# Eight key slabs of the input projection move into the paged-attention stage, and each ring slab becomes one transfer

## What is computed

```python
h = h + 0.5 * swiglu_1(rms_norm(h))              # d_ff 5632
u = rms_norm(h) @ w_in                           # q | k | v | conv value and gate
A = differential attention with ALiBi, 8 heads   # prompt, and samples over paged K and V
B = GLU -> causal depthwise conv (31 taps) -> group LayerNorm -> swish
h = h + concat(A, B) @ w_out
h = h + 0.5 * swiglu_2(rms_norm(h))
h = h + (p @ w_ple_proj) * sigmoid(rms_norm(h) @ w_ple_gate)
y = rms_norm(h)                                  # k, v and conv state are outputs too
```

## Time and profile before

| | us |
|---|---|
| median of 3 runs (2712.27 to 2714.64) | 2712.81 |
| the profiled execution, its own time | 2711.31 |
| its span, from the first to the last instruction | 2709.5 |
| first FFN and the 16 dense slabs of `w_in` | 0 to 1066 |
| attention stage | 1066 to 1514.7 |
| output projection, second FFN, the rest | 1514.7 to 2709.5 |

### The profile page before, as it was taken

One profiled execution on the slowest core, in us unless ns is written; L12 is line 12 of the kernel. 1 busy time (PEld: TensorE's weight loads), 2 busy tenths in 40 slices (PEclk: granted clock), 3 DMA queues, 4 the chain that ended last, 5 costly groups with the idle time before them and its releaser, 6 DMA issues.

```text
span 2709.5 us, 49989 instructions
## 1 busy us (share of the span) xinstructions
PE 2611.9 (96%) x20082; PEld 2542.3 (94%) x20082; DVE 1497.4 (55%) x2082; ACT 942.0 (35%) x1075; POOL 354.3 (13%) x630
## 2 busy tenths in 40 slices
PE   7999999999999999988887899999999999999997
PEld 7999999999999999977775899999999999999997
DVE  5555555555555644467786345555555555555655
ACT  5222322223222332354555433222222222222433
POOL 2000000000000120066865010000000000000323
PEclk9999999999999999999999999999999999999998
DMA  5444444444444455799999844444444444444342
GB/s 231 156 143 152 155 141 153 146 149 154 145 149 152 142 185 200 284 377 365 377 375 382 305 155 144 152 150 145 155 147 147 154 142 153 151 143 155 140 145 81
DMA packets 92112, 506.37 MB, mean 187 GB/s; under 512 B 10401, under 2 KB 10402, under 8 KB 51298
## 3 DMA queue, kind: packets, MB, share of 16 engines
q1 hardware_dynamic: 90866, 496.59, 50.5%
q0 software_dynamic: 1136, 8.32, 0.9%
HBM read 495.63 MB, written 9.23 MB: 186 GB/s over the span
## 4 chain that ended last, share of the span: by engine, by line
PE 89%; DMA 3%; ACT 2%; SPq 2%; issue 2%; POOL 1%; DVE 1%; POOLq 0%; DVEq 0%; ACTq 0%
PE bank L1589 26%; PE bank L1590 26%; PE bank L1591 26%; PE bank L1675 2%; PE bank L1677 2%; PE bank L1676 2%; DMA raw<-k_pool 2%; PE bank L1715 1%; PE bank L1764 1%; SPq L427 1%; POOL ssq L518 1%; SPq L422 1%; PE bank L1741 1%; ACT x_hi L666 1%; DMA raw<-v_pool 1%
## 5 line engine op out<-in xcount | busy, mean ns | idle before, releaser
L1589 PE MATMUL bank<-x_hi,w_hi 128*128 128x320 f32 x3584 | 1111.6, 310 | 17.0 <-DVE w_lo L1046 10.9
L1590 PE MATMUL bank<-x_lo,w_hi 128*128 128x320 f32 x3584 | 1109.9, 310 | 0.0
L1591 PE MATMUL bank<-x_hi,w_lo 128*128 128x320 f32 x3584 | 1109.7, 310 | 0.0
L1037 DVE TENSOR_TENSOR w_lo<-raw,w_hi 128x2048 fp32r<-128x2048 f32 x309 | 707.7, 2290 | 305.8 <-ACT w_hi L648 291.0
L648 ACT CAST w_hi<-raw 128x2048 fp32r<-128x2048 f32 x294 | 559.6, 1903 | 838.2 <-PE bank L1591 838.2
L1589 PEld LDWEIGHTS bank<-x_hi,w_hi 128*128 128x128 f32 x3584 | 674.9, 188 | 19.0 <-issue 13.6
L1590 PEld LDWEIGHTS bank<-x_lo,w_hi 128*128 128x128 f32 x3584 | 675.1, 188 | 0.2
L1591 PEld LDWEIGHTS bank<-x_hi,w_lo 128*128 128x128 f32 x3584 | 674.9, 188 | 0.0
L1589 PE MATMUL bank<-mid_hi,w_hi 128*128 128x320 f32 x1408 | 435.3, 309 | 1.0 <-DVE w_lo L1037 1.0
L1591 PE MATMUL bank<-mid_hi,w_lo 128*128 128x320 f32 x1408 | 435.1, 309 | 0.0
L1590 PE MATMUL bank<-mid_lo,w_hi 128*128 128x320 f32 x1408 | 435.1, 309 | 0.0
(11 more groups left out here) (215 smaller groups left out, 2011.7 us busy)
## 6 DMA issues: line engine op xcount, KB each, us to landing
raw<-slabs_ffn SPq DMA_DIRECT2D x264, 1024.0 KB, 4.7
raw<-k_pool SPq DMA_DIRECT2D x128, 512.0 KB, 6.5
raw<-v_pool SPq DMA_DIRECT2D x128, 512.0 KB, 6.4
raw<-slabs_in SPq DMA_DIRECT2D x48, 512.0 KB, 7.8
raw<-slabs_ple SPq DMA_DIRECT2D x18, 1024.0 KB, 4.8
raw<-slabs_in SPq DMA_DIRECT2D x16, 1024.0 KB, 4.8
raw<-slabs_out SPq DMA_DIRECT2D x16, 1024.0 KB, 4.8
h<-x_t SPq DMA_DIRECT2D x4, 640.0 KB, 8.1
```

What stands on the lines that cost most here:

```text
L1037: vt.tensor_tensor(w_lo[n % 2][:, :, :], raw[n % 4][:, :].rearrange("p (k n) -> p k n", n=P), w_hi[n % 2][:, :, :].bitcast(F32), ALU.subtr ...
L1589: mm(out, w_hi[w2][:, t, :], xh, start=start, stop=False)
L1590: mm(out, w_hi[w2][:, t, :], xl, start=False, stop=False)
L1591: return mm(out, w_lo[w2][:, t, :], xh, start=False, stop=stop)
```

## The change

The dense part of `w_in` keeps only the 8 query slabs (`N_PRE` = 8). The 8 key slabs become the slabs of iteration 0, the 8 value slabs those of iteration 1, two a step, and the convolution and the prompt heads start at iteration 2: `position` counts from there, so that triple c = 0 begins at (2, 0), and block 7 is gated at (7, 3) and not at (6, 3). Iteration 1 therefore has `score(1, q)`, two slabs, the value transposes, `turn(0, q)` and `weigh(0, q)`. The banks of slabs alternate between D_BANK and G_BANK, and value tiles are transposed into H_BANK alone. The casts of finished convolution blocks and heads for the output projection move from iteration 7 to iteration 8, and block 7 gets a piece of its own, `conv_c`, after the split of the first `w_out` slab. That slab ("O") is loaded behind all values and no longer ahead of the last two. GpSimd's key output and `queries(2)`, `queries(3)` shift with the rest. In the ring a slab is loaded by one DMA of 8 KB per partition, with one wait; SP sets the second semaphore of the slot itself.

```diff
-N_PRE = 16
+N_PRE = 8
...
-    if it == 0:
-        return (2 * q, 2 * q + 1)
-    c, r = divmod(4 * (it - 1) + q, PERIOD)
-    return (8 + 2 * c + r,) if c < 8 and r < 2 else ()
+    if it < 2:
+        return (8 * it + 2 * q, 8 * it + 2 * q + 1)
+    c, r = divmod(4 * (it - 2) + q, PERIOD)
+    return (16 + 2 * c + r,) if c < 8 and r < 2 else ()
...
-                if it == NB and q == GROUPS - 1:
-                    order.append(("O", 0))
                 order += [("V", KV_SLOTS * (it - 1) + 2 * q + e) for e in range(2)]
-    return order
+    return order + [("O", 0)]
...
-                    for e in range(2):
-                        slot_free(n, e)
-                        sp.dma_start(ring[slot][:, 1024 * e:1024 * e + 1024],
-                                     slabs_in[N_PRE + at, :, 1024 * e:1024 * e + 1024]
-                                     ).then_inc(ring_in[slot][e], 16)
+                    slot_free(n, 1)
+                    sp.dma_start(ring[slot][:, :], slabs_in[N_PRE + at, :, :]).then_inc(ring_in[slot][0], 16)
+                    sp.sem_inc(ring_in[slot][1], 16)
...
-            pool.wait_ge(evacuated, E(S_IN + 15))
+            pool.wait_ge(d_read, HEADS)
             pool.dma_start(k_t, kT[:, :, :]).then_inc(stored, 16)
...
                     if (it, q) == (NB, 3):
                         sample_upper(0, "sample_a")
                         slab_upper(0)
+                        conv_upper(7, 8, "conv_c")
...
                     if (it, q) == (NB, 3):
+                        conv_swish(7)
                         sample_lower(0, "sample_a")
                         slab_lower(0)
+                        conv_lower(7, 8, "conv_c")
...
+            for q in range(GROUPS):
+                score(1, q)
+                if q:
+                    turn(0, q)
+                slab_half(8 + 2 * q, 0)
+                if q == 0:
+                    turn(0, q)
+                slab_half(8 + 2 * q, 1)
                 if q:
                     v_turn(2 * q - 1)
-                v_slab(2 * q + 1)
+                slab_whole(9 + 2 * q)
                 v_turn(2 * q)
+                if q < GROUPS - 1:
+                    weigh(0, q)
+                if q == 1:
+                    turn(0, "new")
+            score_new(1)
             v_turn(7)
-            score_new(0)
-            for it in range(1, NB + 1):
+            weigh(0, 3, (0,))
+            weigh_new(0)
+            weigh(0, 3, (1,))
+            for it in range(2, NB + 1):
```

More of the change, by code:

```diff
@@ L609, in _ @@
             queries(2)
+            queries(3)
             for c in range(8):
                 sample_taps(c)
-                if c in (0, 1, 2, 4, 5):
-                    queries({0: 3, 1: 4, 2: 5, 4: 6, 5: 7}[c], c + 1)
+                if c in (0, 1, 2, 4):
+                    queries({0: 4, 1: 5, 2: 6, 4: 7}[c], c + 1)
             pool.wait_ge(ln_done, 8)
@@ L728, in _ @@
                     root(1)
-            with act.Fori(1, 3) as i:
-                for j in range(4):
-                    split_next(S_IN, i, j)
             for j in range(3):
-                split_next(S_IN, 3, j)
+                split_next(S_IN, 1, j)
             def exp_tables():
@@ L744, in half_up @@
                 e = n % 2
-                act.wait_ge(ring_in[slot][e], full)
+                act.wait_ge(ring_in[slot][0], full)
                 if n < WBUF:
@@ L760, in v_copy @@
                 nc.scalar.copy(vtok[:, :, P * j:P * j + P],
-                               (H_BANK if j % 2 else G_BANK)[:, 0:3 * P].rearrange("p (a n) -> p a n", n=P)
+                               H_BANK[:, 0:3 * P].rearrange("p (a n) -> p a n", n=P)
                                ).then_inc(vtok_done, 1)
@@ L893, in _ @@
                 slab_up(2 * q + 1)
+                slab_up(2 * q + 2)
+            exp_scores(0, (0,))
+            for q in range(GROUPS):
+                if q == 2:
+                    copy_ET(0, "new")
+                slab_up(9 + 2 * q)
+                copy_ET(0, q)
+                exp_scores(0, ((1, 4), (2,), (3,), ())[q])
                 if q:
                     v_copy(2 * q - 1)
-                slab_up(2 * q + 2)
+                slab_up(10 + 2 * q)
                 v_copy(2 * q)
             v_copy(7)
-            exp_scores(0, (0,))
-            for it in range(1, NB + 1):
+            exp_scores(1, (0,))
+            for it in range(2, NB + 1):
                 b = it - 1
@@ L1161, in _ @@
                 for j in range(4):
-                    split_next(S_IN, i, j)
+                    if not (i == 1 and j == 3):
+                        split_next(S_IN, i, j)
                     if i == 0 and j == 2:
@@ L1168, in _ @@
                         query_tile(i, j)
[L1169 to L1175, removed]
             def tables():
@@ L1403, in _ @@
                 slab_low(2 * q + 1)
-                read_v(2 * q)
+                read_k(2 * q)
                 slab_low(2 * q + 2)
-                read_v(2 * q + 1)
+                read_k(2 * q + 1)
             read_new(0)
             maxima(0)
+            for q in range(GROUPS):
+                if q == 0:
+                    slab_low(9)
+                read_scores(1, q)
+                if q:
+                    slab_low(9 + 2 * q)
+                read_v(2 * q)
+                slab_low(10 + 2 * q)
+                read_v(2 * q + 1)
+            inverse_sums(0)
+            read_new(1)
+            maxima(1)
             dve.wait_ge(state_in, 16)
@@ L1650, in _ @@
                     sum_features(1)
-            with pe.Fori(1, 4) as i:
-                for j in range(4):
-                    pe.wait_ge(evacuated, E(S_IN + 4 * i + j - 4))
-                    dense(S_IN + 4 * i + j, j, j)
+            for j in range(4):
+                pe.wait_ge(evacuated, E(S_IN + j))
+                dense(S_IN + 4 + j, j, j)
             pe.wait_ge(consts, 2)
@@ L1678, in half_of, with slab_half, slab_whole @@
                 m.then_inc(half_mm, 1)
-            def v_slab(j):
-                if j >= 2:
-                    pe.wait_ge(d_read, j - 1)
-                for e in range(2):
-                    half_of(2 * j + e, (O_BANK if j % 2 else D_BANK)[:, 0:NTOK])
+            def slab_half(k, e):
+                if e == 0 and k >= 2:
+                    pe.wait_ge(d_read, k - 1)
+                half_of(2 * k + e, (G_BANK if k % 2 else D_BANK)[:, 0:NTOK])
+            def slab_whole(k):
+                slab_half(k, 0)
+                slab_half(k, 1)
             def conv_half(n):
                 if n % 2 == 0:
-                    c = (n // 2 - HEADS) // 2
+                    c = (n // 2 - 2 * HEADS) // 2
                     pe.wait_ge(d_read, n // 2)
@@ L1694, in v_turn @@
             def v_turn(j):
-                pe.wait_ge(d_read, j + 1)
-                if j >= 2:
-                    pe.wait_ge(vtok_done, j - 1)
-                elif j == 1:
+                pe.wait_ge(d_read, HEADS + j + 1)
+                if j:
+                    pe.wait_ge(vtok_done, j)
+                else:
                     pe.wait_ge(cchain, 6)
-                out = H_BANK if j % 2 else G_BANK
                 for a, t0 in enumerate((0, P, NTOK - P)):
-                    e = nc.tensor.transpose(out[:, P * a:P * a + P], tmp[j % 2][:, t0:t0 + P], ident[:, :])
+                    e = nc.tensor.transpose(H_BANK[:, P * a:P * a + P], tmp[j % 2][:, t0:t0 + P], ident[:, :])
                 e.then_inc(v_turned, 1)
@@ L1747, in o_part, with weigh @@
                 return O_BANK[32 * j:32 * j + 32, at:at + P]
-            def weigh(b, g):
-                if g == 0:
-                    if b == 0:
-                        pe.wait_ge(d_read, HEADS)
-                    else:
-                        pe.wait_ge(o_read, 2 * b)
+            def weigh(b, g, parts=(0, 1)):
+                if g == 0 and b:
+                    pe.wait_ge(o_read, 2 * b)
                 pe.wait_ge(et_done, 10 * b + TURN_AT[g] + 2)
-                for e2 in range(2):
+                for e2 in parts:
                     values = arrived(("V", KV_SLOTS * b + 2 * g + e2))
```

111 lines of the change are left out of this document (61 added, 50 removed).

## The result

The changed kernel takes 2718.22 us (median of 12 runs, 2716.12 to 2722.82), the kernel before 2713.81 in the same runs (12, 2709.54 to 2717.46): ratio 1.0020, 95% interval 1.0013 to 1.0028. That is 4.4 us slower, where 2712.0 was forecast. The profiled execution took 2716.81 us, its span is 2715.0; before, 2711.31 and 2709.5.

What follows compares the result with a forecast made beforehand. TensorE was taken to bound the dense part and iteration 0, DMA transfers the attention after it. Terms -55.6 - 2.5 + 80.9 - 2 + 1.5 - 23.1 = -0.8 us gave a median of 2712.0, range 2699 to 2722.

Steps and rivals of the forecast that it cites:

- The start of attention: With the key slabs out of the dense part, attention starts at 1010.4 and not 1066.01: -55.6 us.
- iteration 1: The value slabs' iteration, new in attention: TensorE sets the pace in steps of 19.7 us, +80.9 us in all.
- its sign of being wrong: In iteration 8, ScalarE's serial stretch being shorter or longer than 12 us would show the forecast wrong.
- The single transfer: Ring slabs behind iteration 1, loaded by one DMA of 8 KB per partition: +1.5 us, with ends of -6 and +7.
- both rivals built on it: Ring slabs: one transfer fills the queue, -10.5, 2702, chance 0.18; or its first half is late, +9, 2722, chance 0.25.
- the one in which the transfers alone set the end: Tail: block 7's taps do not hold it, the last landing does; -42 there, sum -20, 2693 us, chance 0.07.
- the rival at 2722: Ring slabs: ScalarE's upper half waits for the whole slab, TensorE behind it; +4.7 up to +9 us, chance 0.25.
- term 1: Key slabs leave the dense part: -55.6 us, with two query copies of about 0.24 and waits, 0.8 us, exposed.
- term 6: Tail, block 7's gating to output projection: GpSimd's taps 29.3 plus 21.0 us behind them, 50.3 against 73.4, -23.1.
- iteration 0: Key slabs replace value slabs, without value transposes: bare steps of 16.3 us, 66.1 in all against 68.64, -2.5.
- The head start: Iterations 2 to 7: the ring's loads run ahead, worth 0 to 4.2 us; -2 taken as the middle.
- the seven microseconds: The ring's head start before iteration 2, from a place no longer held by the last value slab; one more entry costs 2.8.

Runs made afterwards that it cites:

- 1: The changed kernel with each ring slab's transfer split again into two DMAs of 4 KB per partition: 2719.88 us, ratio 1.0026 to the kernel before.
- 2: The kernel before with only its 24 ring slabs loaded by single transfers: 2712.67 us, ratio 1.0002.
- 12: The changed kernel with VectorE's subtractions kept apart from GpSimd's query copies and block 7's taps: 2713.62 us, ratio 1.0000 to the kernel before.
- 4: The changed kernel with block 7's chain put behind the last weigh, last combine and sample sums on every queue: 2715.55 us, ratio 1.0008 to the kernel before.
- 5: The changed kernel with TensorE multiplying half a key slab before the first score: 2716.51 us, ratio 1.0012 to the kernel before.
- 6: On top of 4, block 7 comes last in the output projection's sum, the variance inside the first slab: 2707.36 us, ratio 0.9968 to the kernel before.
- 7: As 6, but block 7's mean stands ahead of the last weigh and the variance behind it: 2706.56 us, ratio 0.997 to the kernel before.
- 8: As 7, with the start of 5 added: 2702.62 us, ratio 0.9962 to the kernel before.
- 9: As 8, with the last 15 of block 7's 31 sample taps moved to VectorE: 2700.81 us, ratio 0.9957 to the kernel before.
- 3: The changed kernel with GpSimd doing only 8 of block 7's 31 sample taps, the others left out: 2711.74 us, ratio 1.0001 to the kernel before.
- 11: The kernel before with block 7 last in the output projection's sum and its last 15 sample taps on VectorE: 2716.52 us, ratio 1.0012.

## Why the prediction missed

**What held.** The start of attention came within 2 us of its forecast and iteration 1 within 1, in steps of 19.3 to 19.8 us with TensorE full. The mean waits for GpSimd's last tap (12.31 us; 14 forecast) and ScalarE's serial work comes behind it, 10.6 us from the root to `O_n`, where the forecast's items add up to 11.2 and its sign of being wrong names 12. The single transfer is worth nothing (1, 2), so both rivals built on it fall, as does the one in which the transfers alone set the end: TensorE stands idle with a share of 0.29. The measured time lies between the forecast and the rival at 2722, inside the stated range, but by another mechanism: that is luck.

**The step that failed** is the same in two terms: durations of GpSimd were carried over as constants. "Two copies of about 0.24" (term 1) came from a moment when VectorE was not subtracting two SBUF tensors, and "the taps on GpSimd take 29.3 whatever the ring does" (term 6) overlooked that the change moves the heads' lower parts into just these taps. The copies cost 1.7 us more, the taps 2.2. Behind the idle time that the copies lengthen, the forecast put the cost of the lower clock at nothing. It is 1.7 us, the miss of iteration 0, which took 66.2 without it (1, 12); its later steps took 16.14, less than the 16.3 forecast. Together 5.6 of the 6.6 us. Both delays of GpSimd repeat: all ten profiles of the changed kernel and its variants but 12 have copies of 1.08 and 1.12 us, and where GpSimd does all 31 taps beside VectorE's (the changed kernel, 1, 4 to 8) they took 31.2 to 32.5 us. Experiment 12 takes these causes away, and 4.6 us of the median come back. The sign was there: the tap of 1.67 us stands in the same timeline of GpSimd as the two ends of the 29.3.

**The head start** of -2 was not seen (+0.8 with the transfer), and can't be judged: from the start of iteration 2 to block 7's first tap the eleven profiles of the changed kernel and its variants took 304.3 (9) to 313.8 us (12), among them 307.4 (changed) and 309.6 (1), the same program there apart from the transfer in 1. Why it varies by 9 us is open. No row shown gives the seven microseconds from which the forecast worked.

**Why slower and not level.** The tail's gain has a floor. The change takes the transfers off the end of the attention, and what comes to light is first block 7's chain through GpSimd (3: 6.5 us), then ScalarE's order (3, 9). With the block moved last and its mean where TensorE waits little, the kernel with the same move of slabs is 0.4% faster than the kernel before (9). Of its edits only the order of the blocks is shown to gain (6 against 4). In the kernel before the order and the split of the taps bring nothing (11); the other two edits were not tried there. Not tried: 12 together with 9, and ScalarE's copies of `ET` ahead of its table loads.

## What to carry to other kernels

When work is moved, read again the duration of every instruction that gets a new neighbour: here a VectorE subtraction held GpSimd up until its end, and a row from another moment doesn't price that. When a move takes the bound off a stretch, list the chains that were hidden there, with their lengths, and reorder them together with the move. A row that is three times its siblings' mean, like the 1.67 us tap of the kernel before, names a mechanism before the change does.

## What the runs showed of the hardware

**GpSimd stands still beside a VectorE subtraction.** Query copies of 0.23 us took 1.08, 1.12 and 1.29, and taps of 0.44 took 1.49 and 2.47, each up to the end, within 0.3 us, of one or two VectorE instructions of 1.2 us with two SBUF inputs; apart from them they took 0.23 and at most 0.62 (12). By the Trainium skill (SBUF — State Buffer, SBUF: two separate sides) a VectorE instruction with two SBUF inputs and a GpSimd instruction that reads SBUF contend for one pair of ports, which the first to start holds for its whole instruction, and the other waits. The traces agree that GpSimd waits for VectorE's end, in both places. Which came first they don't show: by its row the tap of 1.67 us of the kernel before starts 0.23 us ahead of the subtraction.

**The lower clock after a short idle time is not certain.** After 2.73 us of idle time the same 32 matmuls took 2.61 to 3.62 us in six profiles and 1.93 in one (1); after 0.99 us they took 1.93 (12). After 1.50 us the granted clock fell too, a microsecond into the work (5).

**Two transfers or one made no measurable difference**, 16 of the slabs going at a DMA share of 0.97 to 0.98 and 8 at 0.76 to 0.78: ratios to the kernel before of 1.0002 for one against two (2) and of 1.0026 against 1.0020 for two against one (1). By the fixed part of about 2.0 us a transfer for which the prediction names the Trainium skill (DMA: Bandwidth & Descriptors, Anatomy of one DMA), the 24 slabs of experiment 2 would have gained 48 us, an estimate from that page's figure, if transfers were served one after another. The measurement decides against that; the page fits transfers that GpSimd issues, and these are SP's.
